# A one-core decoder trunk: where the first expert's token rows are read from, and when

## The reference, cut to what matters

```python
def swiglu(x, w_gate, w_up, w_down):
    return (jax.nn.silu(x @ w_gate) * (x @ w_up)) @ w_down

def moe_ffn(x, router_w, w_gate, w_up, w_down):
    logits = (x @ router_w).astype(F32)
    top_val, top_idx = lax.top_k(logits, TOP_K)          # TOP_K = 2, N_EXPERTS = 8
    gates = jax.nn.softmax(top_val, axis=-1)
    combine = jnp.sum(jax.nn.one_hot(top_idx, N_EXPERTS) * gates[..., None], axis=-2)
    out = jnp.zeros(x.shape, F32)
    for e in range(N_EXPERTS):
        out = out + combine[..., e:e + 1] * swiglu(x, w_gate[e], w_up[e], w_down[e])
    return out
# layer 1: x = layer_norm(ALPHA * x + moe_ffn(x, ...), ln2_g, ln2_b)
```

## Time and profile before

| | us |
|---|---|
| runs | 1607.96, 1607.57, 1605.96 |
| median | 1607.57 |
| profiled execution, span of its instructions | 1605.6 |
| TensorE busy in the span | 1554.7 (97%) |
| VectorE busy | 1264.8 (79%) |
| ScalarE busy | 928.3 (58%) |
| POOL busy | 107.5 (7%) |

### The profile page before, as it was taken

The page is one execution under the profiler, slowest core; times in us unless marked ns, Lnnn a source line. Parts: engine busy times, 40 slices in busy tenths (PEclk is TensorE's granted clock), DMA queues, the critical chain, the costliest instruction groups (busy, mean ns, idle before and its releaser), DMA issues.

```text
span 1605.6 us, 23005 instructions
## 1 busy us (share of the span) xinstructions
PE 1554.7 (97%) x8872; PEld 1252.0 (78%) x8872; DVE 1264.8 (79%) x1203; ACT 928.3 (58%) x772; POOL 107.5 (7%) x127
## 2 busy tenths in 40 slices
PE   8998999999999898999999999999999999999995
PEld 6767688888787757888888888888888888888883
DVE  7995755444549767888888888888888888888995
ACT  1253144344205524777777777777777777777773
POOL 0001193000000203000000000000000000000101
PEclk9999999999999999999999999999999999999998
DMA  8430488775443114999999999999999999999992
GB/s 324 159 130 4 163 308 301 276 279 193 157 159 117 70 53 176 395 394 382 395 392 351 396 394 347 397 393 348 396 393 348 397 392 348 396 390 365 391 387 94
DMA packets 190309, 471.74 MB, mean 294 GB/s; under 512 B 7616, under 2 KB 11840, under 8 KB 189184
## 3 DMA queue, kind: packets, MB, share of 16 engines
q1 hardware_dynamic: 186208, 453.70, 76.1%
q0 software_dynamic: 2880, 12.90, 2.2%
q10 hardware_dynamic: 1152, 4.19, 0.6%
HBM read 463.42 MB, written 25.17 MB: 304 GB/s over the span
## 4 chain that ended last, share of the span: by engine, by line
PE 84%; DVE 10%; issue 3%; ACT 2%; DMA 1%; ACTq 0%; SPq 0%; DVEq 0%
PE ps L1579 45%; PE ps L1590 23%; PE ps L1552 4%; PE ps L1965 3%; PE ps L1652 1%; DVE lo L1098 1%; DVE arena L1018 1%; ACT hi L650 1%; PE ps L1559 1%; DVE arena L1036 1%; DVE arena L1053 1%; DMA arena<-in_w_in 1%; ACT arena L709 0%; PE ps L1869 0%; PE ps L1571 0%
## 5 line engine op out<-in xcount | busy, mean ns | idle before, releaser
L1098 DVE TENSOR_TENSOR lo<-arena,hi 128x2048 fp32r<-128x2048 f32 x378 | 869.9, 2307 | 206.1 <-ACT hi L650 205.1
L650 ACT ACTIVATE hi<-arena 128x2048 fp32r<-128x2048 f32 x378 | 724.0, 1920 | 352.2 <-PE ps L1579 225.4
L1579 PE MATMUL ps<-hi,xg 128*128 128x512 f32 x1760 | 543.7, 390 | 1.9 <-DVE xg L1104 1.3
L1579 PEld LDWEIGHTS ps<-hi,xg 128*128 128x128 f32 x1760 | 329.0, 188 | 72.5 <-DVE lo L1098 3.6
L1579 PE MATMUL ps<-lo,xg 128*128 128x512 f32 x880 | 342.5, 389 | 0.0
L1590 PE MATMUL ps<-hi,hTe 128*128 128x512 f32 x896 | 283.9, 398 | 2.2 <-DVE hTe L1128 2.2
L1579 PEld LDWEIGHTS ps<-lo,xg 128*128 128x128 f32 x880 | 165.2, 188 | 34.5
L1590 PEld LDWEIGHTS ps<-hi,hTe 128*128 128x128 f32 x896 | 164.8, 189 | 34.9 <-DVE lo L1098 2.6
L1590 PE MATMUL ps<-lo,hTe 128*128 128x512 f32 x448 | 175.7, 392 | 0.0
L1579 PE MATMUL ps<-hi,xs 128*128 128x512 f32 x512 | 158.3, 390 | 3.2 <-issue 2.1
L1552 PE MATMUL ps<-arena 128*128 128x256 f32 x544 | 121.5, 385 | 3.2 <-DMA arena<-in_w_in 2.2
(11 more groups left out here) (371 smaller groups left out, 1291.2 us busy)
## 6 DMA issues: line engine op xcount, KB each, us to landing
arena<-in_mg SPq DMA_DIRECT2D x112, 1024.0 KB, 7.6
arena<-in_mu SPq DMA_DIRECT2D x112, 1024.0 KB, 7.6
arena<-in_md SPq DMA_DIRECT2D x112, 1024.0 KB, 7.3
arena<-in_w_in SPq DMA_DIRECT2D x7, 2048.0 KB, 10.6
arena<-in_wg SPq DMA_DIRECT2D x14, 1024.0 KB, 5.2
arena<-in_wu SPq DMA_DIRECT2D x14, 1024.0 KB, 5.2
arena<-in_wd SPq DMA_DIRECT2D x14, 1024.0 KB, 5.2
xg_rows<-in_zeros SPq DMA_DIRECT2D x17, 512.0 KB, 6.9
```

What stands on the lines that cost most here:

```text
L650: af(hi[r % PARTS][:, :], raw[r % RAWS], ACT.Copy).then_inc(hi_ready, 1)
L1098: tt(lo[r % PARTS][:, :], raw[r % RAWS], hi[r % PARTS][:, :].bitcast(F32), ALU.subtract)\
L1579: ins = mm(ps[:, (4 if w == "G" else 4 + nb) + b, :], tok[a][:, kk * nt + b * P:kk * nt + (b + 1) * P], tiles_of(part[r % PARTS], w)[:, k, ...
```

## The change

A plain copy of x, `x_rows` (256 rows of 1024), is stored to DRAM by SP in two DMAs as soon as each block of x is normed. The indices of expert 0's tokens come from two TensorE products of `pick` with a constant column of token numbers; VectorE writes them as `row_of[:, 8:9]`. POOL gathers the 128 rows from `x_rows` straight into `xg_in` by one indirect DMA, ahead of its four scatters. SP no longer waits for the scatters ahead of the stream; it waits for them only before it loads the tokens of expert 1 and later. TensorE turns the tokens after piece 3 block 0 rather than after block 1, and the instruction L1453 is split in two halves around `tokens_low(1)`, which moves ahead of `low_part` of piece 5. Some signals are merged (`nA_exp` into `s5_step`, `lg_psum` and `pos_psum` into `route_psum`, `rows2_ready` into `rows_ready`). The constant table grows by two columns and `row_of` by one.

```diff
-CW = C_REV + 12
+C_TOK = C_REV + 12
+CW = C_TOK + NB
...
+    for n in range(NB):
+        c[:, C_TOK + n] = n * P + np.arange(P)
...
-        row_of = sb("row_of", 8, U32)
+        row_of = sb("row_of", 9, U32)
...
-            def tokens_of(i, turned=None):
+            def tokens_of(i, turned):
...
-                if turned is not None:
-                    sp.wait_ge(xg_psum, turned)
+                sp.wait_ge(x_scattered, 64)
+                sp.wait_ge(xg_psum, turned)
                 sp.dma_start(xg_in, rows).then_inc(xg_loaded, 16)
...
             first_pieces(1, *expert_weights(0))
-            sp.wait_ge(x_scattered, 64)
-            tokens_of(0)
+            for b in range(NB):
+                sp.wait_ge(x_ready, NB * 2 + b + 1)
+                sp.dma_start(x_rows[b * P:(b + 1) * P, :], x[:, b, :]).then_inc(x_stored, 16)
             stream(0)
...
+            pool.wait_ge(x_stored, 16 * NB)
+            pool.wait_ge(rows_ready, 2)
+            pool.indirect_dma_start(xg_in, None, x_rows, bass.IndirectOffsetOnAxis(ap=row_of[:, 8:9], axis=0))\
+                .then_inc(xg_gathered, 16)
             pool.wait_ge(xg_zeroed, 16 * FILLS)
-            pool.wait_ge(rows_ready, 1)
...
             low_part(0, PARTS)
             most = dve.value_load(count_i[0:1, 0:1], min_val=0, max_val=T)
+            dve.wait_ge(route_psum, 3)
+            v_.tensor_copy(row_of[:, 8:9], ps[:, 0, 24:25]).then_inc(rows_ready, 1)
             low_part(0, PARTS + 1)
+            dve.wait_ge(half_step, 1)
+            dve.wait_ge(gate_silu, FC + 1)
+            tt(hh[:, 0:512], ps[:, 6, :], sg[:, 0:512], ALU.mult).then_inc(half_step, 1)
+            tokens_low(1)
             dve.wait_ge(piece_used, NP + 4)
-            dve.wait_ge(gate_silu, FC + 1)
-            tt(hh[:, :], ps[:, 6:8, :].rearrange("p a n -> p (a n)"), sg[:, :], ALU.mult).then_inc(h_ready, 1)
+            tt(hh[:, 512:1024], ps[:, 7, :], sg[:, 512:1024], ALU.mult).then_inc(h_ready, 1)
             low_part(0, PARTS + 2)
-            tokens_low(1)
             low_part(0, PARTS + 3)
...
             first_inward(1, 1).then_inc(piece_used, 1)
-            for r in (2, 3):
-                first_inward(r, 0)
-                first_inward(r, 1).then_inc(piece_used, 1)
-
+            first_inward(2, 0)
+            pe.wait_ge(pick_ready, 1)
+            for b in range(NB):
+                ins = mm(ps[:, 0, 24:25], pick[:, b, :], cst[:, C_TOK + b:C_TOK + b + 1], start=(b == 0), stop=(b == 1))
+            ins.then_inc(route_psum, 1)
+            first_inward(2, 1).then_inc(piece_used, 1)
+            first_inward(3, 0).then_inc(half_step, 1)
             tokens_turned(None, 16)
+            first_inward(3, 1).then_inc(piece_used, 1)
+            pe.wait_ge(half_step, 2)
             pe.wait_ge(h_ready, FC + 1)
-            pe.wait_ge(pick_ready, 1)
```

More of the change, by code:

```diff
@@ L149, with build @@
 O_KV, O_KG, O_KD, O_UP, O_WT, O_VP, O_O, O_ST = 3072, 4608, 5376, 6144, 6912, 7680, 8448, 3072
-def build(nc, x_in, w_in, w_out, consts, params, s5_b, glu_w, ln, wg, wu, wd, mg, mu, md, zeros, xg_rows, y_rows, out):
+def build(nc, x_in, w_in, w_out, consts, params, s5_b, glu_w, ln, wg, wu, wd, mg, mu, md, zeros, xg_rows, y_rows, x_rows, out):
     ctx = ExitStack()
@@ L329, in build @@
                                                                             "g_ready", "tg_ready"))
-        nA_exp = sem("nA_exp")
         gs_psum, gs_evac, gs_dve, gs_exp = (sem(n) for n in ("gs_psum", "gs_evac", "gs_dve", "gs_exp"))
@@ L346, in build @@
             sem(n) for n in ("gate_silu", "h_ready", "ht_psum", "ht_hi", "ht_lo", "down_part"))
-        lg_psum, gate_exp_in, gate_exp, sel_ready, pos_psum, route_ready = (
-            sem(n) for n in ("lg_psum", "gate_exp_in", "gate_exp", "sel_ready", "pos_psum", "route_ready"))
+        route_psum, gate_exp_in, gate_exp, sel_ready, route_ready = (
+            sem(n) for n in ("route_psum", "gate_exp_in", "gate_exp", "sel_ready", "route_ready"))
         xg_zeroed, rows_ready, x_scattered, x_scaled, xg_loaded = (
@@ L352, in build @@
         ye_ready, y_stored, y_all = sem("ye_ready"), sem("y_stored"), sem("y_all")
-        pick_ready, rows2_ready, more_added = sem("pick_ready"), sem("rows2_ready"), sem("more_added")
+        pick_ready, more_added = sem("pick_ready"), sem("more_added")
         pick_psum, pickT_ready = sem("pick_psum"), sem("pickT_ready")
@@ L359, in build @@
         last_sum = sem("last_sum")
+        x_stored, half_step, xg_gathered = sem("x_stored"), sem("half_step"), sem("xg_gathered")
         dve_step, act_step, pool_step = sem("dve_step"), sem("act_step"), sem("pool_step")
@@ L629, in _ @@
                         .then_inc(y_gathered[b], 16)
-            pool.wait_ge(rows2_ready, 1)
+            pool.wait_ge(rows_ready, 3)
             pool.wait_ge(y_all, 1)
@@ L731, in _ @@
                     af(s5s[:, 0:16], par[:, PO["ldt"]:PO["ldt"] + 16], ACT.Exp).then_inc(s5_step, 1)
-                    af(nA, par[:, PO["alog"]:PO["alog"] + 12], ACT.Exp).then_inc(nA_exp, 1)
+                    af(nA, par[:, PO["alog"]:PO["alog"] + 12], ACT.Exp).then_inc(s5_step, 1)
                     act.wait_ge(tail_loaded, 16)
@@ L986, in s5_parameters @@
                 ts(gbh[:, :], par[:, PO["gb"]:PO["gb"] + 4], 0.5, None, ALU.mult).then_inc(glu_bias, 1)
-                dve.wait_ge(nA_exp, 1)
+                dve.wait_ge(s5_step, 2)
                 step.then(ts(nA, nA, -1.0, None, ALU.mult))
@@ L1399, in b8 @@
                 return a.unsqueeze(2).to_broadcast([P, 2, NE])
-            dve.wait_ge(lg_psum, 1)
+            dve.wait_ge(route_psum, 1)
             step.then(v_.tensor_copy(lg, ps[:, 0, 0:16].rearrange("p (b e) -> p b e", b=2)))
@@ L1420, in _ @@
             dve.wait_ge(sel_ready, 1)
-            dve.wait_ge(pos_psum, 1)
+            dve.wait_ge(route_psum, 2)
             rank = ps[:, 1, 0:16].rearrange("p (b e) -> p b e", b=2)
@@ L1477, in _ @@
             step(v_.tensor_copy(row_of[:, 4:6], rt[:, 126:128]))
-            v_.tensor_copy(row_of[:, 6:8], rt[:, 128:130]).then_inc(rows2_ready, 1)
+            v_.tensor_copy(row_of[:, 6:8], rt[:, 128:130]).then_inc(rows_ready, 1)
             experts(0)
@@ L1565, in tokens_turned @@
             def tokens_turned(n, loaded):
-                pe.wait_ge(xg_loaded, loaded)
-                if n is not None:
+                if n is None:
+                    pe.wait_ge(xg_gathered, loaded)
+                else:
+                    pe.wait_ge(xg_loaded, loaded)
                     pe.wait_ge(xg_lo, n)
@@ L1676, in expert @@
                     if (w, j, p) == ("U", FC - 1, 0):
-                        tokens_turned(i + 1, i * 16 + 32)
+                        tokens_turned(i + 1, i * 16 + 16)
                 if entries is OPENING:
@@ L2052, in _ @@
                              start=(k == 0), stop=(k == KT - 1))
-            ins.then_inc(lg_psum, 1)
+            ins.then_inc(route_psum, 1)
             first_inward(0, 1).then_inc(piece_used, 1)
@@ L2060, in _ @@
             mm(ps[:, 1, 16:24], C("ones"), sel_[:, 0:8], start=True, stop=False)
-            mm(ps[:, 1, 16:24], C("ones"), sel_[:, 8:16], start=False, stop=True).then_inc(pos_psum, 1)
+            mm(ps[:, 1, 16:24], C("ones"), sel_[:, 8:16], start=False, stop=True).then_inc(route_psum, 1)
             first_inward(1, 1).then_inc(piece_used, 1)
-            for r in (2, 3):
-                first_inward(r, 0)
-                first_inward(r, 1).then_inc(piece_used, 1)
+            first_inward(2, 0)
+            pe.wait_ge(pick_ready, 1)
+            for b in range(NB):
+                ins = mm(ps[:, 0, 24:25], pick[:, b, :], cst[:, C_TOK + b:C_TOK + b + 1], start=(b == 0), stop=(b == 1))
+            ins.then_inc(route_psum, 1)
+            first_inward(2, 1).then_inc(piece_used, 1)
+            first_inward(3, 0).then_inc(half_step, 1)
             tokens_turned(None, 16)
+            first_inward(3, 1).then_inc(piece_used, 1)
+            pe.wait_ge(half_step, 2)
             pe.wait_ge(h_ready, FC + 1)
-            pe.wait_ge(pick_ready, 1)
             for q in range(4):
@@ L2147 @@
         args.append(nc.dram_tensor(name, (ROWS, D), F32, kind="Internal").ap())
+    args.append(nc.dram_tensor("x_rows", (T, D), F32, kind="Internal").ap())
     out = nc.dram_tensor("out_0", (1, T, D), F32, kind="ExternalOutput").ap()
```

## The result

| | before | after |
|---|---|---|
| median, us | 1607.42 (8 runs) | 1612.97 (8 runs) |
| profiled execution: time, span | -, 1605.6 | 1613.23, 1611.4 |

Ratio 1.0039, 95% interval 1.0027 to 1.0051: the change costs 6.3 us (4.3 to 8.2) of the 1607.57 that the prediction started from, 1613.8. The medians alone differ by 5.6 us. The forecast was 1610.0 with a range to 1613.4.

What follows compares the result with a forecast made beforehand. TensorE was taken to bound the kernel (84% of the chain), with room only from 633.3 to 639.8 us. Earlier rows -0.75 plus scaling 3.4 gave +2.65 on 1607.57, 1610.2, stated as 1610.0; range 1605.6 to 1613.4.

Steps and rivals of the forecast that it cites:

- rival 2: Gather lands 7.3 us after its instruction, at 636.3; with the lock +6, 1613.6 us; chance 0.2.
- the mark: TensorE's start of piece 7 at 648.05, 0.6 us after VectorE has it ready; the change is measured against it.
- 3.3 us before they are used: At TensorE's transposes: data of the xg_rows read are there 3.3 us before use, because VectorE is late too.
- Index products, copy, start and length of the gather: Products 0.45 us, VectorE's copy some 0.3, gather starts at 626.8, its instruction ends at 629.0.
- I take 3.5: Gathered rows land 3.5 us after the gather's instruction ends, at 632.5, with 631.3 and 636.3 as ends.
- the estimate of 3.2 us: Gather's start to landing alone, 512 KB, from the skill's fit; by it the rows land about 631.2.
- -0.75: Start of piece 7 from the earlier rows: 647.3, 0.75 us before 648.05, without the scaling's cost.
- G + 14.8: VectorE's path from the rows' landing (G, 632.5) to the start of piece 7, at 647.3.
- The scaling and the lock, 3.4: POOL's scaling holds the shared SBUF port and delays piece 6's low part by 3.4 us; bounds 1.3 and 3.4.
- Rival 1: The scaling does not hurt (shared port, or it fits where VectorE reads PSUM): 1605.7 to 1608.1 us; chance 0.27.
- The other edits: SP's stores, earlier pieces 7 to 9, SP's later wait, merged signals, constant columns: 0; split hh some 0.1 us, in cover.
- The cover of "slack" behind piece 7: Behind piece 7 VectorE needs 2.36 us a piece and TensorE 2.74: nothing more lost, nothing won back.

Runs made afterwards that it cites:

- Run 1: The changed kernel, with SP waiting for the gather to land before it loads piece 10: ratio 1.0043 to the kernel before, median 1613.3 us.
- run 8: The changed kernel with the old route for the rows (scatters first, SP reads rows back, then streams; no gather), new TensorE and VectorE order kept: ratio 1.0031.
- Run 10: The changed kernel with transposes behind piece 3 block 1 as before, scaling moved to ScalarE, stream left free: ratio 0.9993, 1606.59 us.
- run 7: The changed kernel with the old order of TensorE and VectorE, all else as changed: ratio 1.0035.
- run 3: The changed kernel without POOL's scaling of x by ALPHA and the wait for it: ratio 1.0029, median 1611.02 us.
- run 6: The changed kernel with piece 10 held until the gather landed and the scaling moved from POOL to ScalarE: ratio 0.9993, 1606.66 us.
- run 9: The changed kernel with piece 10 held, scaling on ScalarE, and the index products moved ahead of piece 2: ratio 0.9992, 1606.27 us.
- run 4: The kernel before without POOL's scaling and the wait for it: ratio 0.9999.
- run 5: The kernel before, unchanged, run again for a second profile: span 1601.6 us.
- run 2: The changed kernel with SP waiting for the gather before piece 7, so the whole stream is held: ratio 1.0036.

## Why the prediction was wrong, step by step

The sign and the two mechanisms were in it, the sum was not: +2.65 forecast, +6.3 measured, and rival 2 (late gather, +6) was what happened. That its sum comes so near is in part luck: it has 0.6 us too much for the landing (3.8 for 3.2) and 0.6 for the scaling (3.0 for 2.4), and nothing for the clock, which took 1.7. Its own sum is 1613.6, while the range was closed at 1613.4.

- **What bounds it, the 0.6 us margin at piece 7, the mark: right.** The start of piece 7 carries the difference in all runs, but for the half clock behind a long stop. One reading beside it is wrong: the rows of before were not there "3.3 us before they are used". TensorE took them at once (2.29 us of waiting for them), ScalarE's part of the turned tokens ended at 637.8 in the same timeline, and VectorE's began at 638.06. So the parts waited some 0.3 us, no more:

```profile
636.75 1.02 ACT L655 ACTIVATE xg<-ps 128x1024 fp32r<-128x1024 f32 x1 [6.84 <-PE ps L1571]
```

```profile
638.06 1.21 DVE L1104 TENSOR_TENSOR xg<-ps,xg 128x1024 fp32r<-128x1024 f32 x1
```

- **Index products, copy, start and length of the gather: right.** The products took 0.35 us for 0.45, the instruction 2.29 for 2.2 with VectorE's `lo` in its way, and the start was 24.06 from piece 0, less 2.95, 21.1, for 21.4.
- **The landing, "I take 3.5": this is the step that failed.** It was 6.7 after the instruction's end. I had the bytes right for the scatters (the last landed 35.1 us from piece 0 on the scale, for a bound of 34.4), and did not use them for the gather: with SP's 2.1 MB on the way from before it and the scatters behind it, it had the earlier trace rows for its row and not the earlier trace rows. Run 1 shows it: without SP's pieces, 5.8 us for 9.0. What the Trainium skill (DMA: Bandwidth & Descriptors, on arbitration) says of taking turns between queues may hold, but the estimate of 3.2 us from its fit is for a transfer alone, and no run here had the gather alone: its own scatters were always behind it. Counted from the gather's start at 626.8, 3.2 us would also have been 630.0, and not the 631.2 that the prediction gives. The landing of 7.3 was in the prediction as an end, with a chance of 0.2.
- **What a late landing costs: under-sized.** I let TensorE wait without any price beyond the wait. An idle time of 4.5 us was followed by half clock, 1.0 us more on the transposes and 0.7 on piece 3 block 1. The sum of the four terms: -0.75, +3.2 for the landing, +1.7 for the clock, +2.4 for the port is 6.55, against 6.1 on the scale and 6.3 measured.
- **The new order of TensorE: not priced by itself.** I took the transposes' new place as given and asked only when the rows come. With before's landing, G = 635.6, the prediction's own path (G + 14.8) gives +2.4; run 8 shows that this order by itself costs 5 us, 2.5 of them the half clock. Run 10 shows that with before's order a gather of 9.3 us costs nothing. The piece that was moved behind the wait had been its cover.
- **The scaling and the lock, 3.4: right in kind, 2.4 in this run.** The hold itself was 3.3 to 3.5 us again: two `lo` that ended at 649.25 and need 4.71 could have begun at 644.5, 3.3 after POOL's start at 641.25; the first stretched instruction of run 1 gives 3.5. But 0.9 us of it passed before VectorE came to its `lo`. Runs 1 and 7 are worse, 4.4 to 4.8 us, because there a second hold of 1.5 to 1.6 us follows behind a small instruction. The statement that the pair of ports is held for the whole instruction is in the Trainium skill (SBUF — State Buffer, on its two sides). The runs agree in part: an instruction that had begun first was not stretched, and POOL's grew instead (7.25 us in run 7, beside a `lo` of 2.29). They do not agree on the length, 3.4 of the 5.39 us at first, nor on one block: in run 1 an instruction came through between a wait of 3.3 and one of 1.5 us.
- **Rival 1 (it does not hurt): refuted by the stretched `lo` of the changed profile and by run 7 against run 10** (run 3 alone is not clear of noise).
- **"The other edits", 0:** nothing speaks against it; runs 6 and 10 carry them all, stores of x included, at 0.9993.
- **The cover of "slack" behind piece 7: right,** nothing is won back from there to the end; but in runs 1 and 7 the stop of about 4 us at piece 7 adds 1.8 us of half clock, which I had no term for.

The causes do not add: the late landing in the new order costs 4.7 us alone (run 3), the scaling on POOL in the old order 6.7 (run 7 against run 10), and the two together 6.3. Both end in front of piece 7. And with the rows earlier, VectorE was among its small instructions when the scaling began (run 1). That is why undoing one of them seemed to show that it did not matter. That the loss at the transposes is one of cover is shown by runs 8 and 10; that runs 6, 9 and 10 beat the kernel before, by 0.2 to 0.8 us in the medians, is not shown, their intervals take in 1.

## What to carry to other kernels

When a transfer's consumer is moved ahead of other work, that work was its cover: price the move by the latest landing in the trace, not by the likeliest, and the clock that falls behind the wait too. Take bytes in flight on all queues for every transfer of a stretch, also for the first. And where two delays end in front of the same wait, remove them together before judging either: one alone gave 0 and under 2 us, both gave 7.

## What was not expected of the hardware

- A POOL instruction over 128x2048 (5.4 us) stretched VectorE's instructions of 0.15 to 0.35 us to 2.9 and 3.7 us. The second one stretched in run 1 has one operand of 128x128 in SBUF beside its column of scalars (0.28 to 1.75).
- TensorE's clock was at half in the router's stretch in 9 of 13 profiles, at full in 4, with the same instructions ahead of it. It fell while the logits ran (32 matmuls of 128x8: 4.34 us in the changed profile, 3.47 in before). It costs 2.95 us, and it is one of several such stretches: two profiles of before without it still differ by 4.0 us in span, with half clock elsewhere in the longer one. Runs of before went from 1602.7 us at a mean clock of 0.996 to 1613.3 at 0.989.
- After some 2 us of idle time at the transposes the clock fell in runs 4 and 7 (idle 2.20 and 2.01 us, transposes 1.92 and 1.98) and not in before, run 5 and run 10 (idle 2.29, 2.15 and 2.11 us, transposes 1.1). The two that fell had the router's stretch at half clock, the other three at full; why this should matter is not shown. After an idle time of 3.9 to 4.8 us it fell every time, in the changed profile and runs 1, 2, 3, 7 and 8.
